# Hybrid decoder step: masked score levels of a prompt head added in pairs on VectorE ahead of TensorE's output sum

## The reference, cut to what matters

```python
def hgrn2_chunked(q, k, v, logf, s0):
    # S_t = diag(f_t) S_{t-1} + k_t v_t^T ; o_t = S_t^T q_t
    def step(s, inp):
        qb, kb, vb, gb = inp
        G = jnp.cumsum(gb, axis=1)
        o_inter = jnp.einsum('bthk,bhkv->bthv', qb * jnp.exp(G), s)
        diff = G[:, :, None] - G[:, None, :]
        decay = jnp.exp(jnp.where(causal, diff, -jnp.inf))
        scores = jnp.einsum('bthk,btshk->btsh', qb, decay * kb[:, None])
        o_intra = jnp.einsum('btsh,bshv->bthv', scores, vb)
        ...
        return s_new, o_inter + o_intra
```

## Time and profile before

| | us |
|---|---|
| median of 3 runs | 2047.96 |
| lowest, highest | 2038.48, 2048.18 |
| the profiled execution, its own time | 2054.8 |
| its span, first to last instruction | 2053.0 |
| TensorE busy | 1885.0 (92%) |
| VectorE busy | 1367.9 (67%) |
| ScalarE busy | 1047.5 (51%) |
| mean granted TensorE clock | 0.933 of 2.4 GHz |

### The profile page before, as it was taken

The page is one execution under the profiler, slowest core; times in us unless marked ns, Lnnn a source line. Parts: engine busy times, 40 slices in busy tenths (PEclk is TensorE's granted clock), DMA queues, the critical chain, the costliest instruction groups (busy, mean ns, idle before and its releaser), DMA issues.

```text
span 2053.0 us, 26002 instructions
## 1 busy us (share of the span) xinstructions
PE 1885.0 (92%) x10017; PEld 1628.5 (79%) x10017; DVE 1367.9 (67%) x1215; ACT 1047.5 (51%) x917; POOL 63.3 (3%) x69
## 2 busy tenths in 40 slices
PE   6989887999889989786999999999999999999995
PEld 4988766999888978674887887878878788787884
DVE  3635544444345344544787988879888798887986
ACT  3442212333233443213577676766767667676674
POOL 2002010000000011100000000000000000000000
PEclk9997968999999969768899999999999999999997
DMA  7441114444452421114799998989989999999992
GB/s 228 144 136 24 34 36 147 130 144 122 117 187 90 151 57 32 27 36 143 259 349 318 350 369 311 356 324 346 358 316 348 330 343 360 317 347 331 344 354 92
DMA packets 267757, 452.11 MB, mean 220 GB/s; under 512 B 41242, under 2 KB 102930, under 8 KB 267688
## 3 DMA queue, kind: packets, MB, share of 16 engines
q1 hardware_dynamic: 265824, 447.51, 63.4%
q0 software_dynamic: 1600, 3.46, 0.7%
q10 hardware_dynamic: 264, 0.17, 0.1%
HBM read 440.14 MB, written 10.97 MB: 220 GB/s over the span
## 4 chain that ended last, share of the span: by engine, by line
PE 84%; DVE 9%; ACT 3%; issue 2%; DMA 1%; DVEq 0%; SPq 0%; POOL 0%; ACTq 0%
PE ps L1411 15%; PE ps L1412 15%; PE ps L1883 10%; PE ps L1406 7%; PE ps L1407 7%; PE ps L1897 5%; PE ps L1485 3%; PE ps L1797 3%; PE ps L1592 2%; PE ps L1577 2%; PE ps L1760 2%; PE ps L1750 1%; DVE cvt L975 1%; PE ps L1812 1%; ACT spH L550 1%
## 5 line engine op out<-in xcount | busy, mean ns | idle before, releaser
L1302 DVE TENSOR_TENSOR spL<-ring,spH 128x2048 fp32r<-128x2048 f32 x339 | 771.9, 2292 | 152.7 <-ACT spH L809 152.5
L809 ACT ACTIVATE spH<-ring 128x2048 fp32r<-128x2048 f32 x339 | 648.5, 1915 | 163.1 <-PE ps L1897 101.0
L1411 PE MATMUL ps<-spH,XH 128*128 128x512 f32 x896 | 357.8, 399 | 1.5 <-DVE XL L1314 1.5
L1412 PE MATMUL ps<-spH,XL 128*128 128x512 f32 x896 | 352.5, 393 | 0.0
L878 DVE TENSOR_TENSOR spL<-ring,spH 128x2048 fp32r<-128x2048 f32 (+1 forms) x74 | 158.2, 2147 | 246.0 <-ACT spH L550 245.9
L1406 PE MATMUL ps<-hnH,spH 128*128 128x320 f32 x928 | 275.4, 311 | 13.0 <-DVE hnL L896 7.1
L1407 PE MATMUL ps<-hnL,spH 128*128 128x320 f32 x928 | 274.0, 310 | 0.0
L550 ACT ACTIVATE spH<-ring 128x2048 fp32r<-128x2048 f32 (+1 forms) x74 | 132.4, 1797 | 248.0 <-PE ps L1485 108.7
L1883 PE MATMUL ps<-spL,XH 128*128 128x512 f32 x896 | 242.5, 392 | 0.0
L1411 PEld LDWEIGHTS ps<-spH,XH 128*128 128x128 f32 x896 | 169.0, 189 | 38.7 <-issue 1.7
L1883 PEld LDWEIGHTS ps<-spL,XH 128*128 128x128 f32 x896 | 168.8, 188 | 37.7
(11 more groups left out here) (319 smaller groups left out, 2175.2 us busy)
## 6 DMA issues: line engine op xcount, KB each, us to landing
ring<-in_w_exp_in_dram SPq DMA_DIRECT2D x227, 1024.0 KB, 7.2
ring<-in_w_exp_out_dram SPq DMA_DIRECT2D x112, 1024.0 KB, 6.9
ring<-in_w_in_dram SPq DMA_DIRECT2D x28, 1024.0 KB, 5.6
ring<-in_w_ffn_in_dram SPq DMA_DIRECT2D x22, 1024.0 KB, 5.1
ring<-in_w_ffn_out_dram SPq DMA_DIRECT2D x16, 704.0 KB, 4.6
ring<-in_w_out_dram SPq DMA_DIRECT2D x8, 1024.0 KB, 5.1
out_dram<-ring SPq DMA_DIRECT2D x32, 256.0 KB, 2.6
ring<-in_state_hgrn_dram SPq DMA_DIRECT2D x16, 256.0 KB, 3.6
```

The costliest lines, as they stand in the source:

```text
L809: A(esplit(j)[0], src, ACT.Copy).then_inc(S("hi_done"), 1)
L1302: V.tensor_tensor(lo, eslot(j)[0], hi.bitcast(F32), ALU.subtract).then_inc(S("split_done"), 1)
L1411: mm(out, x[0], w, start=start, stop=False)
L1412: return mm(out, x[1], w, start=False, stop=False)
```

## The change

The masked scores of a prompt head no longer go to TensorE as eight levels. VectorE waits for its mask product, then adds levels 4 to 7 of `SC` (columns 512 to 1023) to levels 0 to 3 in place, a sum of 128x512, and `sc_done` is raised by this sum. `output` then takes four products for every tile: levels 0 to 3 of `SC`, for the sample tile the four it had before. The eight levels are multiplied by the same `v`, so the sum is the same up to rounding.

```diff
                     if t < 2:
-                        V.tensor_tensor(SCv, ps[:, 2:4, :].rearrange("p b n -> p (b n)"), tabv("mask"), ALU.mult
-                                        ).then_inc(S("sc_done"), 1)
+                        own(V.tensor_tensor(SCv, ps[:, 2:4, :].rearrange("p b n -> p (b n)"), tabv("mask"), ALU.mult))
+                        V.tensor_tensor(SCv[:, 0:512], SCv[:, 0:512], SCv[:, 512:1024], ALU.add).then_inc(S("sc_done"), 1)
...
-                    for v in range(nl + 1):
+                    for v in range(4):
                         m = mm(out, vtk_of(t)[0:n, h * P:(h + 1) * P], flat(SCb[h % 2])[0:n, v * n:(v + 1) * n],
-                               start=v == 0, stop=v == nl and t != 1)
+                               start=v == 0, stop=v == 3 and t != 1)
```

## The result

| | before | changed |
|---|---|---|
| median, us | 2048.07 | 2056.64 |
| lowest to highest, us | 2038.48 to 2055.12 | 2049.75 to 2068.74 |
| executions | 20 | 20 |
| mean granted clock | 0.934 | 0.925 |

The changed kernel takes 1.0044 times as long, 95% interval 1.0027 to 1.006: about 9 us slower, where 10 us faster was forecast and the range ended at 2047. (The mean clock of before is over the 89 executions that ran beside the experiments; their mean time is 2049.3 us.) A ninetieth, at 2170.6 us and a clock of 0.81, was in a second, slower state and is left out everywhere. The profiled execution took 2056.1 us around a span of 2054.3.

The account below looks back on a forecast made before the run. TensorE was taken to bound the kernel, with VectorE on its path at some heads. 6.6 us from the heads plus 3.4 from the clock made 10.0 us off the median 2047.96, so 2038.0 us, range 2033 to 2047.

Parts of the forecast that it names:

- The price of the removal: Output of each prompt head on TensorE: four products, 8 records, fewer, taken as 0.93 us less.
- The price of the addition: VectorE at each prompt head: a 0.69 us sum plus 0.04 us wait, so the mask is handed over 0.74 us later.
- Head by head: Head stage of each layer's mixer, unchanged clock: gains and waits summed over eight prompt heads, 3.3 us a layer.
- the wait of a sample state for L1062 at (1,1): Second sample state before the output of (1,1) waits 0.45 us for the ring addition, leaving 0.48 us gained there.
- The clock: Head stage: one of two half-rate falls of TensorE's clock goes in each layer, 1.7 us a layer, 3.4 in all.
- Sum: Head stages of both layers at an unchanged clock: 6.6 us faster.
- The rule that was set aside: Skill's rule that idle gaps between matmul groups lower TensorE's clock; by it the change loses time; it changed no term.
- the last rival: Between scores and output of (1,2): clock falls in the longer wait and stays down, 12 us slower, 2060; chance 0.09.
- The price of that rival: Half rate through the SSD products, 238 to 267 us, and before: 18.4 us less 6.6, so 12 us slower.
- The cover was thin: Rival: all eight heads wait for their add, 3.0 us gained in two layers, +2 at worst, middle near 2046; chance 0.16.
- The range: Whole kernel: 2033 us with both falls gone to 2047 with the thin cover; only the slow case and part of tails out.
- A term that the text said it couldn't settle: TensorE's clock in the head stage: from 3.4 us a layer more gained to 0.7 a layer more with no fall gone.

Follow-up runs that it names:

- add_at_h0: The changed kernel with addition and four products only at heads (0,0) and (1,0), other heads as before: 0.9975 of before, 5.1 us faster in the mean.
- changed_again: The changed kernel run once more, unaltered, on the chip of the next runs: 1.0058 of before, median 2059.5 us.
- two_halves: The kernel before with mask product and output in two halves, one per PSUM bank, no addition: 0.9932 of before, median 2033.5 us.
- after_fill: The changed kernel with unread products in TensorE's waits for the sum at (0,2), (0,3), (1,2) and (1,3): 0.9971 of before, 7.2 us faster.
- pairs_apart: The kernel before with three unread 128-column products between the two sample states of a pair: 0.9973 of before, 4.7 us faster.
- before_fill: The kernel before with unread products in its waits for the mask at (0,2), (0,3), (1,2) and (1,3): 1.0001 of before.

## Why the prediction was wrong

By its steps:

- *The price of the removal*, 0.93 us a head. Right: the outputs take 1.09 us for 1.98 on the chain, 0.89 less.
- *The price of the addition*, 0.69 + 0.04, handed over 0.74 later. Right: 0.692 us each, with 0.02 us between mask and sum (190.84 + 1.24 to 192.10).
- *Head by head*. Right in layer 0, where it was read. (0,0) and (1,0) don't wait, four heads and (0,1) do, and the wait of a sample state for L1062 at (1,1), set at 0.45, is there with 0.44 of TensorE's idle time:

```profile
PE ps L1626 <- DVE ring L1062: 0.4, 1, 0.4
```

- *The clock: "I take one fall gone in each layer, 1.7 a layer, 3.4 in all"*. **This is the step that failed.** It had the wrong sign. Where one of two falls a layer was to go, the profiled execution after has 17 us at half rate among the prompt heads of layer 0 and about 31 in layer 1 (the stretches above), 48 for 14 before. The change spent 36 us more at half rate in the mean, worth some 13 us by the line through the executions, where the text had counted on 3.4 us back. Sum and clock together, -6.6 + 13 = +6.4, come near the 8.0 that were measured; -6.6 and -3.4 do not.
- *The rule that was set aside.* The prediction named the last rival's place, the wait between the scores of (1,2) and its output, and gave it 0.09, because "1.9 us of waiting inside 224 to 233 left the clock at full". That was one execution. With 2.7 us in layer 0 and 2.2 in layer 1 in the same place, and half the output behind it, the clock fell in both layers of the profile after (at 224 and at 808 us). The runs with filling show that this place and (1,3) make the loss. The Trainium skill ("TensorE: Matmul & The Clock Gate", the section "HAM oscillation — how this bites in real kernels") says that gaps between groups of matmuls bring the clock down and that the next group starts cold. The trace after agrees: 2.35 of 5 us busy at 1.00, then 0.53 for 18 us, though the page's gaps are waits for DMA and longer than the 2.7 us here. The page's section on psum-queue depth-cycling, on short and frequent gaps between groups, fits layer 1 with its four falls.
- *The price of that rival*, 12 us slower, was over the measured 8 to 10, since the clock did rise again before 262 us in layer 0 where it was taken to stay down. As a mechanism it was the right one.
- *The cover was thin*: no. (0,0) and (1,0) stayed free, and add_at_h0 gains.
- *The range.* 2033 to 2047 rested on the head-by-head sum with small terms around it. A term that the text said it couldn't settle should have held the range open on both sides by its size: there were 14 us of half rate among the prompt heads of the profiled execution before, and waits about to grow next to it.

What stays open: what makes a wait of 2.2 us let the clock down in one kernel and one of 2.6 us not at once in another, and where the rest of the falls come from. They differ between executions of one program also ahead of the change: from 145 to 178 us before ran at 0.50, while the same part of changed_again (143 to 171) had 0.88, and that execution is one of its kernel's two fastest. The means over executions carry the argument, not one profile.

## What to carry to other kernels

Taking work off TensorE and putting a shorter operation of another engine in its place can lose time though every price is right: here longer waits let TensorE's clock fall, and the work behind the wait paid. Price a change of this kind at one clock first, then look at what it does to TensorE's standing still, above all at its longest wait, and compare the mean granted clock of many executions with that of before. Cut the wait before cutting the work: handing over half of a result when it is there (two_halves) gained 14 us with no product less, 7 of them foreseen by the sum.

## What the runs showed that I had not expected

- Unread products can make the program faster: 15 us from 52 of them in after_fill, in waits that let the clock fall, 4.7 us from 12 in pairs_apart, by a way not shown, and nothing from 34 in before_fill.
- Two of a layer's four waits carried the whole loss (2042.3 with them filled, 2058.1 with the other two filled, 2059.5 with none).
- Executions of one program differ by 10 to 20 us, and their mean granted clock goes with it: 2049.75 us at 0.929 and 2068.74 at 0.920 for the changed kernel.
